# Seven block products for two more units of every up chunk, and value products one slot earlier

## The reference

```
h = rms_norm(x, norm_mix)
x = x + hybrid_mixer(h, w_in, ...)      # h @ w_in, three attention branches, gates, w_out
h = rms_norm(x, norm_ffn)
x = x + (silu(h @ w_gate) * (h @ w_up)) @ w_down     # 2048 -> 5632 -> 2048
out = rms_norm(x, norm_final)
```

## Time and profile before

| what | value |
|---|---|
| median of 3 runs (range) | 1398.5 us (1398.1 to 1399.4) |
| the profiled execution, time | 1400.08 us |
| its span, first to last instruction | 1398.4 us |
| PE busy | 1386.4 us, 99% of the span |
| DVE busy | 923.2 us, 66% |
| ACT busy | 701.9 us, 50% |
| q1 (weight loads), share of 16 DMA engines | 59.7% |
| mean granted TensorE clock | 0.998 |

### The profile page before, as it was taken

One profiled execution on the slowest core, in us unless ns is written; L12 is line 12 of the kernel. 1 busy time (PEld: TensorE's weight loads), 2 busy tenths in 40 slices (PEclk: granted clock), 3 DMA queues, 4 the chain that ended last, 5 costly groups with the idle time before them and its releaser, 6 DMA issues.

```text
span 1398.4 us, 18555 instructions
## 1 busy us (share of the span) xinstructions
PE 1386.4 (99%) x7344; PEld 1172.5 (84%) x7344; DVE 923.2 (66%) x1189; ACT 701.9 (50%) x912; POOL 45.4 (3%) x70
## 2 busy tenths in 40 slices
PE   9999999999999999999999999999999999999997
PEld 8999977777788888888888989888888898888886
DVE  5455557657655657666788888874446788887554
ACT  7333356656545655465645555543334455545443
POOL 4000000000000110000000000000000000000111
PEclk9999999999999999999999999999999999999999
DMA  7777755545565667556566665565666575667653
GB/s 239 247 217 219 216 140 150 149 139 148 150 184 164 188 200 213 174 164 201 157 182 204 213 184 177 184 216 193 191 185 179 182 221 164 192 190 228 207 188 115
DMA packets 135233, 260.58 MB, mean 186 GB/s; under 512 B 8448, under 2 KB 25408, under 8 KB 134768
## 3 DMA queue, kind: packets, MB, share of 16 engines
q1 hardware_dynamic: 133328, 251.89, 59.7%
q0 software_dynamic: 1792, 7.57, 1.5%
q10 hardware_dynamic: 32, 0.01, 0.0%
HBM read 257.33 MB, written 2.10 MB: 186 GB/s over the span
## 4 chain that ended last, share of the span: by engine, by line
PE 94%; DVE 3%; DMA 1%; ACT 1%; issue 1%; SPq 0%; ACTq 0%; DVEq 0%
PE bank L628 25%; PE bank L629 25%; PE bank L630 25%; PE bank L867 5%; PE bank L869 5%; PE bank L870 5%; PE bank L619 2%; DVE weight_lo_ring L1259 1%; DMA raw_ring<-in_w_up 1%; PE bank L766 1%; PE bank L677 1%; DVE weight_sums_lo L1279 0%; ACT weight_hi_ring L1029 0%; DMA x<-in_x 0%; DVE weight_sums L1268 0%
## 5 line engine op out<-in xcount | busy, mean ns | idle before, releaser
L1259 DVE TENSOR_TENSOR weight_lo_ring<-raw_ring,weight_hi_ring 128x1024 fp32r<-128x1024 f32 (+2 forms) x480 | 581.3, 1220 | 326.6 <-ACT weight_hi_ring L1029 273.0
L1029 ACT ACTIVATE weight_hi_ring<-raw_ring 128x1024 fp32r<-128x1024 f32 (+2 forms) x432 | 448.7, 1051 | 363.4 <-PE bank L630 297.2
L628 PE MATMUL bank<-weight_hi_ring,hT_hi 128*128 128x512 f32 (+2 forms) x768 | 303.3, 395 | 0.0
L629 PE MATMUL bank<-weight_lo_ring,hT_hi 128*128 128x512 f32 (+2 forms) x768 | 296.9, 387 | 0.0
L630 PE MATMUL bank<-weight_hi_ring,hT_lo 128*128 128x512 f32 (+2 forms) x768 | 296.8, 386 | 0.0
L628 PEld LDWEIGHTS bank<-weight_hi_ring,hT_hi 128*128 128x128 f32 x768 | 145.0, 189 | 31.2 <-issue 6.5
L630 PEld LDWEIGHTS bank<-weight_hi_ring,hT_lo 128*128 128x128 f32 x768 | 145.0, 189 | 27.2
L629 PEld LDWEIGHTS bank<-weight_lo_ring,hT_hi 128*128 128x128 f32 x768 | 145.2, 189 | 24.6
L628 PE MATMUL bank<-weight_hi_ring,h2T_hi 128*128 128x512 f32 x352 | 139.6, 397 | 0.6 <-DVE weight_lo_ring L1259 0.5
L629 PE MATMUL bank<-weight_lo_ring,h2T_hi 128*128 128x512 f32 x352 | 139.1, 395 | 0.0
L628 PE MATMUL bank<-weight_hi_ring,actT_hi 128*128 128x512 f32 x352 | 139.0, 395 | 0.0
(11 more groups left out here) (238 smaller groups left out, 1736.5 us busy)
## 6 DMA issues: line engine op xcount, KB each, us to landing
raw_ring<-in_w_in SPq DMA_DIRECT2D x96, 512.0 KB, 3.6
raw_ring<-in_w_gate SPq DMA_DIRECT2D x88, 512.0 KB, 4.5
raw_ring<-in_w_up SPq DMA_DIRECT2D x88, 512.0 KB, 4.3
raw_ring<-in_w_down SPq DMA_DIRECT2D x88, 512.0 KB, 4.6
raw_ring<-in_w_in SPq DMA_DIRECT2D x56, 452.0 KB, 4.2
raw_ring<-in_w_out SPq DMA_DIRECT2D x32, 512.0 KB, 4.6
raw_ring<-in_w_br_c SPq DMA_DIRECT2D x16, 256.0 KB, 4.7
raw_ring<-in_w_br_a SPq DMA_DIRECT2D x16, 256.0 KB, 7.4
```

Source lines behind the costliest of these rows:

```text
L628: pe.matmul(dst, x_hi, w_hi, start=first and k == 0, stop=False)
L629: pe.matmul(dst, x_hi, w_lo, start=False, stop=False)
L1029: act.activation(whi[:, s, :, 0:width(u)], raw[:, s, :, 0:width(u)], ACT.Copy).then_inc(hi_ready, 1)
L1259: dve.tensor_tensor(lo, w, hi.bitcast(F32), ALU.subtract).then_inc(lo_ready, 1)
```

## The change

`SEVEN` goes from five of the eight units of every up chunk to seven (all but j = 7). With it `h2S_hi` and `h2S_lo`, which hold the activation sums, grow from five to seven entries. In the attention stage `VALUES_AT` places the value products six instead of seven slots behind the query-key products of the same piece; as these recur every third slot, the value products of piece i then stand in the slot of the query-key products of piece i+2, right behind them.

```
-SEVEN = (0, 1, 2, 4, 5)
+SEVEN = (0, 1, 2, 3, 4, 5, 6)
...
-VALUES_AT = {soft_slot(i) + 7: i for i in range(N_SOFT)}
+VALUES_AT = {soft_slot(i) + 6: i for i in range(N_SOFT)}
```

## The result

The changed kernel takes 1461.9 us (median) where the kernel before, run beside it on the same chip, takes 1398.9: ratio 1.0445, 95% interval 1.0431 to 1.0459. It is slower by 63 us; forecast were 1463 and +65. Single executions far off from the rest (2758.2 us in one of the four of the changed kernel, 2287.4 in one of the kernel before in a later series) are left out of the numbers here; nothing on record explains them. The profiled execution has a span of 1460.2 us (1398.4 before, so +61.8) and a mean granted TensorE clock of 0.983 (0.998 before).

A forecast was written before the change was run, and what follows sets the result against it. PE bounds the kernel before, but DVE, with 2.0 us to spare per period, would set the pace after the change. 59.7 + 6.0 + 0.9 - 0.5 - 1.0 = +65.1 us gave a median of 1463, range 1436 to 1482.

The forecast's parts named there:

- PE's gain: Up chunks: 22 units turned seven save PE 0.26 us each, 5.8 us if nothing else held PE.
- u6: Up chunks: unit 6 turned seven makes one more 5.72 us DVE pair replacing two plain splits, +3.45 us per chunk.
- u3: Up chunks: unit 3 after seven-product unit 2 leaves DVE waiting for ACT without a filler, +4.77 us per chunk.
- DVE's period: Up chunks: 45.5 us plus 5.0 for the arrival of unit 0's weights, 50.5 against 43.9 before.
- Nine periods: From unit 6 of one up chunk to the next, five and four periods at 6.63 us more: 59.7 us.
- First chunks: Up to unit 6 of each half's first up chunk: +6.0 us without DVE lead, +0.9 with full lead.
- Last chunks: Behind unit 6 of each half's last up chunk: DVE recovers, PE keeps 0.26 us twice, -0.5 us.
- Value products: Attention stage: one entry less into a value group in 9 slots, between 0 and 3.2 us gained, taken as 1.
- a covered arrival: Up chunks: rival in which unit 0's load shows no wait, period 47.8, +40.5 us, 1439; chance 0.17.
- The faster rival: Up chunks: rival in which they stay bound by PE, 1391.7 us; chance 0.05.
- The clock: Up chunks: rival in which new pauses bring PE's clock to 1.2 GHz, up to 1593 us; chance 0.05.
- the main case: Up chunks: DVE sets the period and unit 0's load arrival shows, 1456 to 1480 us; chance 0.63.

The follow-up runs named there:

- e9: Changed kernel with nearly all weight sums left out on DVE (outputs not the reference's): 1390.41 us, ratio 0.9938.
- e10: Kernel before with value products moved and nearly all weight sums left out on DVE (outputs not the reference's): 1395.01 us, ratio 0.9971.
- e2: Kernel before with only unit 6 added to the seven-product units, value products not moved: 1413.12 us, ratio 1.0098.
- e4: Changed kernel with two buffers for the weight sums, so the next unit's sums may always precede the current unit's split: 1421.23 us, ratio 1.0159.
- e5: Changed kernel with 26 otherwise useless transposes filling PE's pause ahead of unit 3: 1459.19 us, ratio 1.0433.
- e6: Kernel of e3 with 26 otherwise useless transposes filling PE's pause ahead of unit 3: 1440.17 us, ratio 1.0288.
- e3: Kernel before with only unit 3 added to the seven-product units, value products not moved: 1443.87 us, ratio 1.0325.

## Why the prediction was right

1. *PE's gain, 5.8.* Shown by e9 against e10: 4.6 between medians, 4.8 between spans (1388.5 and 1393.3). Real, about 1 us smaller than the sum, and not to be had as long as DVE sets the period.
2. *u6, +3.45 per chunk on DVE.* Right: e2's period of 45.73 is the sum with it.
3. *u3, +4.77 per chunk, most of it waiting.* Right to the digit: 5.70 and 5.72 where 5.72 twice was forecast, the wait 1.91 where 1.9 was forecast. e4 shows that it is mostly the wait: the other order gives 3.2 of the 4.8 back in every chunk. The 3.3 forecast for PE's pause ahead of u3 are 3.00 of idle time, 3.27 from start to start; ahead of g7 PE waits 1.11 where 1.5 was forecast, and no wait shows ahead of u0, where about 1 was.
4. *DVE's period, 50.5.* Measured by the starts of L1311: 50.1 to 50.7, but 48.4 and 49.2 for the last of each half. The arrival of u0's load, taken as 5.0, was 4.8: u7's lo part ends at 808.86 + 1.13 + 1.22 = 811.2, and the sums start at 816.02.
5. *Nine periods, 59.7.* Measured 57.3. The missing 2.4 lies in the first half. Half of it is only moved: PE began the first u6 of the half 1.59 us behind DVE's lo part and the last 0.35, so 1.24 us count under step 6 and not here. The other half is about what an arrival of 4.8 in place of 5.0 makes over five periods.
6. *First chunks, +6.0 and +0.9.* Measured +6.66, and +0.6 for the second together with the last chunk of the first half, where 0.64 was forecast. The first is made otherwise than I had it: u6's lo part was there earlier (at 708.96 of the changed kernel's clock, 711.35 without the 2.39 that lie ahead of this stage, where 712.3 was forecast), but PE came 1.6 us behind it. That this is the low clock after u3 fits e5, whose filler keeps the clock up: its first L1311 (L1314 there) starts at 716.60, in the changed kernel at 717.97, 1.0 us later when the 0.36 by which e5 is ahead at the transposes is taken off.
7. *Last chunks, -0.5.* Measured -0.4 for the second half's, where 0.26 was forecast; that of the first half is within the +0.6 of step 6.
8. *Value products, -1.* Measured -1.8, inside the bounds of 0 to 3.2. The -2.4 in the table holds 0.6 of luck, as kernels that are the same up to there differ by that much and more. The term of the sum that was off the most in proportion.

By the spans the sum is 3.3 us too high (65.1 against 61.8), by the medians 1.6. The better figure is luck: of the kernel before, the profiled execution was 1.6 us slower than its median, of the changed kernel it was not.

Of the rivals, a covered arrival is refuted by the idle 2.53 before u0's sums, which a load ends. The faster rival needed the added work to fit into DVE's slack; e9 shows that it would have been right if the sums cost nothing. The clock did fall, in one place per chunk and in nine of eleven chunks, as that rival said; the main case had it at nothing. The Trainium skill's tale of a kernel whose waits for data brought the clock down (TensorE: Matmul & The Clock Gate, section HAM oscillation) is borne out here, with 0.59 in the window behind the pause. But it took less than the slack per period, 46.00 us of busy time in place of the 43.3 that PE needs, out of 50.28, and e5 shows that it is worth about 3 us in all. It does account for one sign that did not come true: PE's waits for L1259 were to be 50 to 60 us and are 43.0 (31.4 in 13 waits of L867, 11.6 in 14 of L628). Part of what was forecast as a pause shows as slower matmuls, and PE is busy for 18.5 us more with 66 matmuls fewer.

What the prediction lacked is the mixed way. It didn't count here because DVE's own was the longest; for u3 alone it did, and that forecast failed by 15 us. So the agreement to 2 us doesn't show that adding up single engines is enough.

## What to carry to other kernels

Fewer matmuls by more elementwise work is a trade between two engines: before making it, add up the second engine's own period from starts in its timeline, waits included, and compare with the first's. Here its slack was 2.0 us per period and the trade asked for 8.2, of which 3.2 was only an order in which it had to wait for a third engine with nothing to do in between. And when several engines pass work around in rings, look for the longest way round over all of them: the period can be longer than that of any one engine, 47.8 us in e6, where the sums for DVE and PE alone were 46.9 and 43.6.

## What was unexpected of the hardware

- One pause of PE was often enough to bring its clock down: idle 3.00 us before u3, then a granted clock of 0.59 over the next 3 us and 0.88 over the 4 after that, while PE was busy without a gap; in e3 it was 0.50 over 6 us. The same pause filled with transposes left it at 1.00. But the same pause unfilled did not always do it: the clock fell behind nine of ten in the changed kernel and six of ten in e3, where the four of the second half left it at 1.00. No row shows what set them apart.
- Two groups of small matmuls side by side instead of apart gave PE 0.20 us per slot (1.78 us over nine, the same to 0.01 in every kept trace), without any matmul less.
- Sums on GpSimd made DVE's splits 9% longer on average (1352 against 1238 ns), 40% where the two ran together, and GpSimd's own operations twice as long.
